# Parameter chain of the state-space part ahead of the feature evictions, upper table levels on VectorE alone

## The chip, the core and the metric

The kernel runs on one core of a Trainium2 chip. The metric is the device time of one launch in microseconds (us). The engines of the core are named as in the profile: PE (TensorE: matrix products and transposes), DVE (VectorE), ACT (ScalarE), POOL (GpSimd) and SP (SyncE, here the issuer of all DMAs). Each runs its own list of instructions in order, and semaphores tie the lists together.

## The reference

One inference step of a one-layer decoder: 256 prompt tokens and 8 x 4 sample tokens, 288 in all, width 1024.

```python
z = rmsnorm(x, norm_g) @ w_in            # [q | k | v | u], each 512 wide
attn = dilated window attention of q, k, v (prompt; samples with a cache of 1024)
dt = exp(log_dt); a_bar = exp((a_re + i a_im) * dt)
b_bar = ((a_bar - 1) / lam) * (b_re + i b_im)
h[t] = a_bar * h[t-1] + b_bar @ u[t];  y[t] = Re(c @ h[t]) + d_skip * u[t]
g = gelu(y); ssm_o = g * sigmoid(g @ w_glu + b_glu)
x = x + [rmsnorm(attn) | rmsnorm(ssm_o)] @ w_out
x = x + moe(rmsnorm(x))                  # top 4 of 32 experts, 1024 -> 2048 -> 1024
y = rmsnorm(x)
```

The state-space part has 32 groups of 16 channels with a complex state of 64 each. All is float32.

## The kernel before

The work is written out by hand, one list for each engine; where two engines meet there is a semaphore `S[...]`, and the order of the lines is the order of the work. `link` makes an engine wait for its own last instruction.

The start. ACT and DVE normalise x into `xn`. PE transposes it in 8 pieces of the width, the "features" j = 0 to 7 (L1036, three transposes each), into four PSUM banks in turn; DVE evicts the even ones (L698), ACT the odd ones (L545), both scaled by `gmx`, into `accT`. So feature j waits for the eviction of feature j − 4. Then PE transposes C and the old states h0 (L1041, L1042, ten transposes) and, when DVE has multiplied the two rows of parameters by dt (L703, L704, semaphore `rows`), the four small parameter rows (L1045, semaphore `prmT`). DVE copies these into `prm` (L707) and reduces the angles to the range of the sine (L708 to L716, semaphore `red`), then evicts h0 (L717) and C (L721, L722). ACT computes the radii (Exp, L550) and cosine and sine (L551, L552, semaphore `exps`).

From there three things run side by side. PE multiplies the features with the four blocks of w_in that give u (`project(0)` to `project(3)`, L1060), and then, in its own order, transposes b_bar (L1070, semaphore `bT_ps`). DVE computes a_bar and b_bar from the parameters (L726 to L754, semaphore `fdone`). POOL builds the angle table `e_tab`, the powers 1 to 128 of the unit factor of a_bar for 16 pairs of groups, by doubling: level L makes 2^L more powers out of the 2^L that are there, with four products, a difference and a sum, on 16 x 2^L elements of each of 128 partitions. POOL does levels 0 to 3 alone (L448 to L458); in levels 4 to 6 POOL does the real part (three operations, L448 to L450) and DVE the imaginary part (L762 to L764), and each level waits for both halves of the one before. Between its levels 5 and 6 DVE copies the transposed b_bar out of PSUM (L771, L772, semaphore `bT`), for which PE waits before the first product of the loop.

The loop over 16 state groups i. PE computes `bu(i)` (b_bar times u, L1082), one turn ahead in two banks; DVE turns it by the table (L786 to L791), runs the scans over time in two halves (L796 to L807) and turns back the low half; POOL turns back the high half (L508 to L513); PE multiplies with C (`c_h(i)`, L1103). Between them PE does the other twelve blocks of the projection, the key and value transposes and the first sample scores. Behind the loop come the attention of prompt and samples, the gated unit, the output projection, the router and the experts, whose 402 MB of weights are fetched in pieces of 1 MB; the first of these loads are issued when the attention is done (`pv`).

Two lines of the angle table on DVE, as they stand before:

```python
for level in (4, 5):
    angle_level(level).then_inc(S["etab_d"], 1)
```

Of the kernel before, what the change touches and what calls it, by code (L numbers as in the profile page):

```python
# [26 lines left out]
ALU = mybir.AluOpType  # L27
ACT = mybir.ActivationFunctionType
# [72 lines left out]
def decoder_step(nc, I, O):  # L101

    with ExitStack() as ctx:
# [85 lines left out]
        def s5_buf(n):  # L189
# [46 lines left out]
            gex ysv b1z b1 b2 etab_p etab_d etab_v gmx con_rest sc osel o_ev yfin  # L236
# [190 lines left out]
        def _(pool):  # L427
# [12 lines left out]
            for level in range(7):  # L440
# [5 lines left out]
                if level >= 5:  # L446
                    pool.wait_ge(S["etab_d"], level - 4)
                link(tt(t1, re, cr, ALU.mult))  # L448
                link(tt(t2, im, ci, ALU.mult))
                ins = tt(e_tab[:, 0, :, m:2 * m], t1, t2, ALU.subtract)  # L450
                if level >= 4:
                    ins.then_inc(S["etab_p"], 1)
                    pool.wait_ge(S["etab_p"], level - 2)
                    continue
                link(ins)
# [3 lines left out]
                if level == 3:  # L459
                    ins.then_inc(S["etab_p"], 1)  # L460
                    pool.wait_ge(S["etab_p"], 1)
                else:
                    link(ins)
# [60 lines left out]
        def _(act):  # L524
# [17 lines left out]
            act.wait_ge(S["gmx"], 16)  # L542
            for n, j in enumerate(range(1, J, 2)):
                act.wait_ge(S["xT_ps"], j + 1)
                A(accT[:, j, :], ps[:, 4 + j % 4, 0:NTOK], ACT.Copy, scale=gmx[:, j:j + 1]).then_inc(S["xT_a"], 1)  # L545
            act.wait_ge(S["prm"], 16 * NPRM)
            A(ld[0:NI, 0:2], ld[0:NI, 0:2], ACT.Exp).then_inc(S["dt"], 1)

            act.wait_ge(S["red"], 1)
            A(prm[:, PA_R, :], prm[:, PA_RD, :], ACT.Exp)  # L550
            A(prm[:, PA_C, :], prm[:, 11, :], ACT.Sin)  # L551
            A(prm[:, PA_S, :], prm[:, 12, :], ACT.Sin).then_inc(S["exps"], 1)  # L552

# [119 lines left out]
        def _(dve):  # L673
# [21 lines left out]
            dve.wait_ge(S["gmx"], 16)  # L695
            for j in range(0, J, 2):
                dve.wait_ge(S["xT_ps"], j + 1)
                ts(accT[:, j, :], ps[:, 4 + j % 4, 0:NTOK], gmx[:, j:j + 1], None, ALU.mult).then_inc(S["xT_d"], 1)  # L698

# [7 lines left out]
            link(dve.tensor_copy(prm[:, 0:4, :], ps[:, 0, 0:64].rearrange("p (a i) -> p a i", a=4)))  # L707
# [8 lines left out]
            ts(two, two, PI_IN, -PI_IN, ALU.min, ALU.max).then_inc(S["red"], 1)  # L716
            link(dve.tensor_copy(h0[:, :, :], ps[:, 1, 0:2 * P].rearrange("p (r n) -> p r n", r=2)))  # L717
# [38 lines left out]
            def angle_level(level):  # L756

                m = 1 << level
                dve.wait_ge(S["etab_p"], level - 3)
                re, im = e_tab[:, 0, :, 0:m], e_tab[:, 1, :, 0:m]  # L760
                t1, t2 = (e_tmp_v[:, a].rearrange("p (i t) -> p i t", i=NI)[:, :, 0:m] for a in range(2))
                tt(t1, re, bc(e_tab[:, 1, :, m - 1:m], [P, NI, m]), ALU.mult)  # L762
                link(tt(t2, im, bc(e_tab[:, 0, :, m - 1:m], [P, NI, m]), ALU.mult))
                return tt(e_tab[:, 1, :, m:2 * m], t1, t2, ALU.add)  # L764

            dve.wait_ge(S["fdone"], 1)
            for level in (4, 5):
                angle_level(level).then_inc(S["etab_d"], 1)
                dve.wait_ge(S["etab_d"], level - 3)
            dve.wait_ge(S["bT_ps"], 1)  # L770
            dve.tensor_copy(bT[:, 0, :], ps[:, 0, :])  # L771
            dve.tensor_copy(bT[:, 1, :], ps[:, 1, :]).then_inc(S["bT"], 1)  # L772
            angle_level(6).then_inc(S["etab_v"], 1)
            dve.wait_ge(S["late"], 16 * 5)

            dve.wait_ge(S["etab_p"], 4)
# [249 lines left out]
        def _(pe):  # L1026
# [5 lines left out]
            for j in range(J):  # L1032
# [4 lines left out]
                ins.then_inc(S["xT_ps"], 1)  # L1037
            pe.wait_ge(S["prm"], 16 * NPRM)
            for r in range(2):
                for b in range(4):  # L1040
                    tp(ps[:, 2 + r, P * b:P * b + P], cnat[:, r, b, :], ident)  # L1041
# [410 lines left out]
```

## Time and profile before

| | |
|---|---|
| device time, three runs | 1430.23, 1430.82, 1434.66 us; median 1430.82 |
| the profiled execution | 1433.22 us, its span from first to last instruction 1431.4 us |
| mean granted clock of TensorE | 0.932 |
| PE busy | 1197.0 us (84%) |
| DVE busy | 574.9 us (40%) |
| ACT busy | 226.4 us (16%) |
| POOL busy | 93.6 us (7%) |
| chain that ended last | PE 61%, DMA 10%, SP's queue 9%, DVE 8% |

Shares over the whole span say little about the start, since most of the span is the experts. The change touches the first 60 us, so the timeline of that stretch is what to read: a row gives the start of an instruction (or of a few alike), its length, the engine and line, and in brackets how long the engine stood idle before it and what released it.

### The profile page before, as it was taken

Reading aid. Unit: us, or ns where it says so; the run is one execution under the profiler, and the core shown is the slowest. Engines: PE = TensorE matmul, PEld = TensorE weight load, DVE = VectorE, ACT = ScalarE, POOL = GpSimd, SP = SyncE. Lnnn points to the kernel's source line nnn. Section 1 sums busy time; section 2 is a strip of 40 time slices with the busy share of each in tenths; the row PEclk is TensorE's granted clock in tenths of the full one; section 3 lists DMA queues with packets and bytes.
Section 4 is the critical chain, followed back from the end, with each engine's and each line's share of the span. In section 5 each row is a group of like instructions: output and inputs, shape, how many; then the busy total and the mean of one; then the engine's idle time right before and its main releaser. Section 6 shows DMA issues by size and latency. Waiting matters only on the chain.

```text
span 1431.4 us, 25686 instructions
## 1 busy us (share of the span) xinstructions
PE 1197.0 (84%) x8896; PEld 477.7 (33%) x8897; DVE 574.9 (40%) x1305; ACT 226.4 (16%) x433; POOL 93.6 (7%) x189
## 2 busy tenths in 40 slices
PE   6998778886998688999889888898998966689965
PEld 4665445534332122333223222333332311223321
DVE  4899622234443233333343333443343322234324
ACT  3002433011111011111111111111111101011112
POOL 1668200000000000000000000000000000000000
PEclk9899878885999999999999999999999988899988
DMA  8225482530479999988978997999639999988893
GB/s 256 102 74 187 158 290 65 231 127 9 173 307 424 424 423 423 424 372 336 423 312 352 391 424 287 423 424 425 272 168 398 423 423 424 424 369 344 349 422 151
DMA packets 77902, 444.94 MB, mean 311 GB/s; under 512 B 16560, under 2 KB 17392, under 8 KB 26640
## 3 DMA queue, kind: packets, MB, share of 16 engines
q1 hardware_dynamic: 77872, 444.56, 76.5%
q8 instruction: 17, 0.28, 0.1%
q14 instruction: 13, 0.11, 0.0%
HBM read 442.02 MB, written 2.51 MB: 311 GB/s over the span
## 4 chain that ended last, share of the span: by engine, by line
PE 61%; DMA 10%; SPq 9%; DVE 8%; issue 7%; DVEq 2%; ACT 1%; POOL 1%; ACTq 0%
PE ps L1355 19%; SPq L402 9%; PE ps L1341 9%; DMA ring<-in_w_moe_dram 7%; PE ps L1364 7%; PE ps L1371 5%; PE ps L1291 3%; PE ps L1383 3%; PE ps L1060 3%; DMA uni<-in_w_moe_dram 2%; PE ps L1379 1%; PE ps L1396 1%; PE ps L1130 1%; DVE uni L1007 1%; PE ps L1328 1%
## 5 line engine op out<-in xcount | busy, mean ns | idle before, releaser
L1355 PE MATMUL ps<-ring,uni 128*32 128x512 f32 x2240 | 253.4, 596 | 10.8 <-DMA ring<-in_w_moe_dram 10.8
L977 DVE TENSOR_TENSOR x<-x,ps 128x1024 f32<-128x1024 f32 x158 | 186.7, 1209 | 6.6 <-PE ps L1341 3.4
L1341 PE MATMUL ps<-uni 64*128 64x512 f32 x632 | 173.6, 655 | 5.2 <-DVE uni L972 2.6
L1371 PE MATMUL ps<-uni 128*32 128x256 f32 x1224 | 92.5, 443 | 85.9 <-issue 85.9
L998 DVE TENSOR_SCALAR uni<-ps 128x256 f32<-128x256 f32 x51 | 21.7, 425 | 341.9 <-PE ps L1355 341.9
L1364 PE MATMUL ps<-ring,uni 128*32 128x512 f32 x1120 | 130.4, 599 | 31.8 <-DVE uni L1007 18.1
L1355 PEld LDWEIGHTS ps<-ring,uni 128*32 128x32 f32 x2240 | 71.4, 110 | 182.3 <-issue 157.1
L654 ACT ACTIVATE uni<-uni 128x256 f32<-128x256 f32 x51 | 21.2, 417 | 539.6 <-DVE uni L998 539.6
L1371 PEld LDWEIGHTS ps<-uni 128*32 128x32 f32 x1224 | 40.9, 123 | 151.9 <-issue 139.0
L1341 PEld LDWEIGHTS ps<-uni 64*128 64x128 f32 x632 | 55.7, 198 | 105.5 <-issue 100.8
L654 ACT ACT_TABLE_LOAD x51 | 65.4, 1283 | 80.5 <-issue 80.1
L987 DVE COPY uni<-ps 128x256 f32<-128x256 f32 x51 | 21.7, 425 | 135.7 <-PE ps L1371 135.7
L1060 PE MATMUL ps<-accT,ring 128*128 128x288 f32 x256 | 68.8, 427 | 0.0
L1364 PEld LDWEIGHTS ps<-ring,uni 128*32 128x32 f32 x1120 | 31.7, 109 | 104.6 <-issue 53.3
L1355 PE MATMUL ps<-tmp,uni 128*32 128x512 f32 x512 | 61.2, 593 | 2.8 <-DMA tmp<-in_w_moe_dram 2.8
L982 DVE TENSOR_TENSOR uni<-con,uni 128x96 f32 (+1 forms) x51 | 13.2, 259 | 122.4 <-issue 122.4
L658 ACT ACTIVATE uni<-ps 128x256 f32<-128x256 f32 x51 | 19.5, 383 | 230.0 <-PE ps L1364 230.0
L1060 PEld LDWEIGHTS ps<-accT,ring 128*128 128x128 f32 x256 | 49.9, 199 | 16.9 <-issue 3.3
L1383 PE MATMUL ps<-kv_rows,uni 128*32 128x512 f32 x408 | 54.6, 607 | 0.0
L1291 PE MATMUL ps<-ring,mixer 128*128 128x512 f32 (+1 forms) x96 | 43.4, 614 | 0.5 <-DVE st L904 0.5
L1007 DVE COPY uni<-ps 128x256 f32<-128x256 f32 x51 | 21.7, 425 | 48.6 <-PE ps L1402 48.6
L991 DVE TENSOR_TENSOR uni<-uni 128x96 f32<-128x96 f32 x204 | 38.5, 251 | 0.0
(317 smaller groups left out, 1172.9 us busy)
## 6 DMA issues: line engine op xcount, KB each, us to landing
ring<-in_w_moe_dram SPq DMA_DIRECT2D x258, 1024.0 KB, 20.2
tmp<-in_w_moe_dram SPq DMA_DIRECT2D x42, 1024.0 KB, 17.8
accT<-in_w_moe_dram SPq DMA_DIRECT2D x21, 1024.0 KB, 19.7
mixer<-in_w_moe_dram SPq DMA_DIRECT2D x21, 1024.0 KB, 21.2
w_glu<-in_w_moe_dram SPq DMA_DIRECT2D x21, 1024.0 KB, 22.8
uni<-in_w_moe_dram SPq DMA_DIRECT2D x21, 1024.0 KB, 24.4
ring<-in_w_in_dram SPq DMA_DIRECT2D x4, 2048.0 KB, 13.0
ring<-in_cache_k_dram SPq DMA_DIRECT2D x8, 1024.0 KB, 5.0
```

The costliest lines, as they stand in the source:

```text
L402: sp.dma_start(slot(turn, k), piece(e + later, k2)).then_inc(landed(turn, k), 16)
L654: A(sig, glu_b, ACT.Sigmoid, scale=ALPHA).then_inc(S["sgm"], 1)
L977: tt(rows(t), rows(t), ps[0:TILES[t][1], b0:b0 + 2, :], ALU.add).then_inc(S["acc"], 1)
L991: ins = tt(selg[:, :, q, :], sel, gb, ALU.mult)
L1007: dve.tensor_copy(mt, ps[:, 3, 0:NQ].rearrange("p (m c) -> p m c", c=P)).then_inc(S["mt"], 1)
L1060: ins = mm(ps[:, 4 + n % 2, 0:NTOK], w_in[:, c // 4, j, P * (c % 4):P * (c % 4) + P], accT[:, j, :], start=(j == 0), stop=(j == J - 1))
L1291: ins = mm(ps[0:n, b0 + 2 * a + c, :], src[:, kb, t0:t0 + n], w_out[:, 4 * a + kb, 512 * c:512 * c + 512], start=(kb == 0), stop=(kb == 3))
L1341: ins = mm(ps[:, b0 + c, :], selT[rows, P * t:P * t + P], y[rows, :], start=True, stop=True)
L1355: ins = mm(hidden(q), xe[:, k % 2, quarter(k // 2)], columns(slot(turn, k), q), start=False, stop=(k == 7), skip_group_check=True)
L1364: ins = mm(ps[quarter(2 * c + m), 4, :], mt[:, m, quarter(k - 8)], slot(turn, k)[:, at:at + 512], start=(k == 8), stop=(k == 11), skip_gro ...
L1371: ins = mm(ps[quarter(q), 2, 0:NQ], sel[:, t, :], h[:, t, NQ * q:NQ * q + NQ], start=(t == 0), stop=(t == 2), skip_group_check=True)
L1383: mm(hidden(q), pick, columns(b1_rows, q), start=True, stop=False, skip_group_check=True)
```

## The change

Four edits. On DVE the even evictions of features move from ahead of the parameter chain to behind the range reduction. On PE the parameter transposes move between features 3 and 4, and C and h0 behind feature 7, with a new semaphore `cps` for DVE's eviction of h0. On ACT the Exp of dt and the Exp of the radii (which gets its own semaphore `prmc`) move ahead of the odd evictions, and cosine and sine between features 3 and 5. In the table, levels 4 to 6 are done whole by DVE, six operations each, behind the copies of b_bar; POOL stops at level 3.

```diff
 # POOL
-            for level in range(7):
+            for level in range(4):
...
-                if level >= 5:
-                    pool.wait_ge(S["etab_d"], level - 4)
                 link(tt(t1, re, cr, ALU.mult))
                 link(tt(t2, im, ci, ALU.mult))
-                ins = tt(e_tab[:, 0, :, m:2 * m], t1, t2, ALU.subtract)
-                if level >= 4:
-                    ins.then_inc(S["etab_p"], 1)
-                    pool.wait_ge(S["etab_p"], level - 2)
-                    continue
-                link(ins)
+                link(tt(e_tab[:, 0, :, m:2 * m], t1, t2, ALU.subtract))
 # ACT
-            act.wait_ge(S["gmx"], 16)
-            for n, j in enumerate(range(1, J, 2)):
+            def features_out(j):
                 act.wait_ge(S["xT_ps"], j + 1)
                 A(accT[:, j, :], ps[:, 4 + j % 4, 0:NTOK], ACT.Copy, scale=gmx[:, j:j + 1]).then_inc(S["xT_a"], 1)
+
             act.wait_ge(S["prm"], 16 * NPRM)
             A(ld[0:NI, 0:2], ld[0:NI, 0:2], ACT.Exp).then_inc(S["dt"], 1)
-
+            act.wait_ge(S["prmc"], 1)
+            A(prm[:, PA_R, :], prm[:, PA_RD, :], ACT.Exp)
+            act.wait_ge(S["gmx"], 16)
+            features_out(1)
+            features_out(3)
             act.wait_ge(S["red"], 1)
-            A(prm[:, PA_R, :], prm[:, PA_RD, :], ACT.Exp)
             A(prm[:, PA_C, :], prm[:, 11, :], ACT.Sin)
             A(prm[:, PA_S, :], prm[:, 12, :], ACT.Sin).then_inc(S["exps"], 1)
+            features_out(5)
+            features_out(7)
 # DVE
-            dve.wait_ge(S["gmx"], 16)
-            for j in range(0, J, 2):
-                dve.wait_ge(S["xT_ps"], j + 1)
-                ts(accT[:, j, :], ps[:, 4 + j % 4, 0:NTOK], gmx[:, j:j + 1], None, ALU.mult).then_inc(S["xT_d"], 1)
...
             ts(two, two, PI_IN, -PI_IN, ALU.min, ALU.max).then_inc(S["red"], 1)
+            dve.wait_ge(S["gmx"], 16)
+            for j in range(0, J, 2):
+                dve.wait_ge(S["xT_ps"], j + 1)
+                ts(accT[:, j, :], ps[:, 4 + j % 4, 0:NTOK], gmx[:, j:j + 1], None, ALU.mult).then_inc(S["xT_d"], 1)
+
+            dve.wait_ge(S["cps"], 1)
             link(dve.tensor_copy(h0[:, :, :], ps[:, 1, 0:2 * P].rearrange("p (r n) -> p r n", r=2)))
...
-                tt(t1, re, bc(e_tab[:, 1, :, m - 1:m], [P, NI, m]), ALU.mult)
-                link(tt(t2, im, bc(e_tab[:, 0, :, m - 1:m], [P, NI, m]), ALU.mult))
-                return tt(e_tab[:, 1, :, m:2 * m], t1, t2, ALU.add)
-
-            dve.wait_ge(S["fdone"], 1)
-            for level in (4, 5):
-                angle_level(level).then_inc(S["etab_d"], 1)
-                dve.wait_ge(S["etab_d"], level - 3)
+                t3, t4 = (e_tmp[:, a, :, 0:m] for a in range(2))
+                tt(t1, re, cr, ALU.mult)
+                tt(t2, im, ci, ALU.mult)
+                tt(t3, re, ci, ALU.mult)
+                link(tt(t4, im, cr, ALU.mult))
+                tt(e_tab[:, 0, :, m:2 * m], t1, t2, ALU.subtract)
+                return tt(e_tab[:, 1, :, m:2 * m], t3, t4, ALU.add)
+
             dve.wait_ge(S["bT_ps"], 1)
             dve.tensor_copy(bT[:, 0, :], ps[:, 0, :])
             dve.tensor_copy(bT[:, 1, :], ps[:, 1, :]).then_inc(S["bT"], 1)
+            dve.wait_ge(S["fdone"], 1)
+            dve.wait_ge(S["etab_p"], 1)
+            link(angle_level(4))
+            link(angle_level(5))
             angle_level(6).then_inc(S["etab_v"], 1)
 # PE
-            for j in range(J):
+            def features(j):
...
+            for j in range(4):
+                features(j)
             pe.wait_ge(S["prm"], 16 * NPRM)
-            for r in range(2):
-                for b in range(4):
-                    tp(ps[:, 2 + r, P * b:P * b + P], cnat[:, r, b, :], ident)
-                tp(ps[:, 1, P * r:P * r + P], h0row[:, r, :], ident)
             pe.wait_ge(S["rows"], 1)
             for a, src in enumerate((par[0:NI, 0:P], par[0:NI, P:2 * P], st_out[0:NI, 0, :], st_out[0:NI, 1, :])):
                 ins = tp(ps[:, 0, NI * a:NI * a + NI], src, ident[0:NI, 0:NI])
             ins.then_inc(S["prmT"], 1)
+            for j in range(4, J):
+                features(j)
+            for r in range(2):
+                for b in range(4):
+                    tp(ps[:, 2 + r, P * b:P * b + P], cnat[:, r, b, :], ident)
+                ins = tp(ps[:, 1, P * r:P * r + P], h0row[:, r, :], ident)
+            ins.then_inc(S["cps"], 1)
```

On DVE, from the last step of b_bar (written into `tmp`) to the first instruction of the loop (reading `ps`), before; `ring` holds the temporaries and b_bar transposed, `uni` the table:

```order
L754 TENSOR_TENSOR tmp<-ring 64x16x16
L762 TENSOR_TENSOR ring<-uni 128x16x16
L763 TENSOR_TENSOR ring<-uni 128x16x16
L764 TENSOR_TENSOR uni<-ring 128x16x16
L762 TENSOR_TENSOR ring<-uni 128x16x32
L763 TENSOR_TENSOR ring<-uni 128x16x32
L764 TENSOR_TENSOR uni<-ring 128x16x32
L771 COPY ring<-ps 128x512
L772 COPY ring<-ps 128x512
L762 TENSOR_TENSOR ring<-uni 128x1024
L763 TENSOR_TENSOR ring<-uni 128x1024
L764 TENSOR_TENSOR uni<-ring 128x16x64
```

And the same place of the changed kernel, up to the middle of level 5:

```order
L753 TENSOR_TENSOR tmp<-ring 64x16x16
L770 COPY ring<-ps 128x512
L771 COPY ring<-ps 128x512
L762 TENSOR_TENSOR ring<-uni 128x16x16
L763 TENSOR_TENSOR ring<-uni 128x16x16
L764 TENSOR_TENSOR tmp<-uni 128x16x16
L765 TENSOR_TENSOR tmp<-uni 128x16x16
L766 TENSOR_TENSOR uni<-ring 128x16x16
L767 TENSOR_TENSOR uni<-tmp 128x16x16
L762 TENSOR_TENSOR ring<-uni 128x16x32
L763 TENSOR_TENSOR ring<-uni 128x16x32
L764 TENSOR_TENSOR tmp<-uni 128x16x32
```

The two copies of b_bar (COPY ring<-ps) moved ahead of levels 4 and 5, and each level has six operations instead of three.

On PE, the start of the changed kernel from feature 3 to the projection (L1068); before, the rows of `par` and `st_out` (the parameter transposes) stand directly ahead of the projection, and no row stands between the features:

```order
L1046 MATMUL ps<-con,par 128x16 x2
L1046 MATMUL ps<-con,st_out 128x16 x2
L1038 MATMUL ps<-con,uni 128x128 x2
...
L1052 MATMUL ps<-con,tmp 128x128 x4
L1053 MATMUL ps<-con,h0row 128x128
L1052 MATMUL ps<-con,tmp 128x128 x4
L1053 MATMUL ps<-con,h0row 128x128
L1068 MATMUL ps<-accT,ring 128x288 x32
```

Features 4 to 7 and the transposes of C (`tmp`) and h0 (`h0row`) now stand between the parameter transposes and the projection.

## Rows read from the trace of the kernel before

**Rows 1.** The chain of waits in order of time: start, us, what.

```profile
45.91 2.08 PE ps L1082 x8
...
103.93 1.07 PE ps L1082 x4
```

**Rows 2.** By stretch: length, busy PE, PEld, DVE, ACT, POOL, clock, DMA.

```profile
44.70:54.80 10.10, 8.89 (x79) 7.59 (x80) 10.07 (x5) 0.00 (x0) 8.79 (x4) 0.50 0.04 14
55.00:105.00 50.00, 50.00 (x199) 33.06 (x197) 47.88 (x122) 4.61 (x10) 28.04 (x62) 1.00 0.16 53
```

**Rows 3.** Timelines of DVE and PE, the loop and its end.

```profile
55.01 0.69 DVE L786 TENSOR_TENSOR ring<-ps,uni 128x512 f32<-128x512 f32 x1 [0.20 <-DVE uni L764]
...
97.75 1.13 PE L1082 MATMUL ps<-uni,ring 32*128 32x256 f32 x4
...
104.43 0.46 DVE L807 TENSOR_TENSOR_SCAN ring<-prm,ring 128x128 f32<-128x128 f32 x1
105.00 0.69 DVE L786 TENSOR_TENSOR ring<-ps,uni 128x512 f32<-128x512 f32 x1
...
160.02 1.02 PE L1103 MATMUL ps<-ring 128*32 128x256 f32 x4 [1.16 <-POOL ring L513]
```

**Rows 4.** Timelines of all engines, 13 to 56 us.

```profile
13.76 6.97 PE L1036 MATMUL ps<-con,uni 128*128 128x128 f32 x24 [13.76 <-DVE uni L693]
...
23.42 0.39 PE L1045 MATMUL ps<-con,par 16*128 16x16 f32 x2 [0.37 <-DVE st_out L704]
23.96 17.57 PE L1060 MATMUL ps<-accT,ring 128*128 128x288 f32 x64
...
25.72 0.42 DVE L717 COPY ring<-ps 128x256 f32<-128x256 f32 x1
...
27.48 0.20 ACT L552 ACTIVATE prm<-prm 128x16 f32<-128x16 f32 x1
...
32.69 0.49 DVE L754 TENSOR_TENSOR tmp<-ring 64x256 f32<-64x256 f32 x1
...
37.87 0.45 POOL L458 TENSOR_TENSOR uni<-tmp 128x128 f32<-128x128 f32 x1
...
41.36 1.04 PE L1070 MATMUL ps<-con,tmp 128*128 128x128 f32 x8
...
44.56 0.69 DVE L771 COPY ring<-ps 128x512 f32<-128x512 f32 x1
...
45.77 2.92 DVE L762 TENSOR_TENSOR ring<-uni 128x1024 f32<-128x1024 f32 x1
45.91 2.08 PE L1082 MATMUL ps<-uni,ring 32*128 32x256 f32 x8 [3.51 <-DVE ring L772]
...
51.56 3.25 DVE L764 TENSOR_TENSOR uni<-ring 128x1024 f32<-128x1024 f32 x1
```

**Rows 5.** SP's small loads issued between 9 and 11 us.

```profile
L303 SPq DMA_DIRECT2D tmp<-in_ssm_c_im_dram x2: 507/507/507, 9.4 to 9.9; - x2
...
DMA to landing us min/median/max: 2.5/2.6/3.1
```

**Rows 6.** Durations: timelines, and one group by line (count, busy us, mean ns).

```profile
14.78 0.52 DVE L698 TENSOR_SCALAR accT<-ps,vec 128x288 f32<-128x288 f32 x1 [1.17 <-PE ps L1036]
...
40.94 0.69 DVE L762 TENSOR_TENSOR ring<-uni 128x512 f32<-128x512 f32 x1
41.55 1.53 DVE L763 TENSOR_TENSOR ring<-uni 128x512 f32<-128x512 f32 x1
...
51.38 9.75 PE L1060 MATMUL ps<-accT,ring 128*128 128x288 f32 x32
...
56.40 0.43 DVE L790 TENSOR_TENSOR ring<-ring 128x256 f32<-128x256 f32 x1
...
62.12 4.15 PE L1060 MATMUL ps<-accT,ring 128*128 128x288 f32 x16
...
L896 DVE TENSOR_TENSOR uni<-mixer 128x1152 f32<-128x1152 f32 x1 | 1.4, 1358 | 0.0
```

More of the change, by code:

```diff
@@ L235, in decoder_step @@
             wo_ps x2 ss3 ms3 rt3 h hT_ps lg rout posps posm cntr gT_ps gT b2ps acc0 chain_a chain_v chain_p
-            gex ysv b1z b1 b2 etab_p etab_d etab_v gmx con_rest sc osel o_ev yfin
+            gex ysv b1z b1 b2 etab_p etab_v prmc cps gmx con_rest sc osel o_ev yfin
             sel selg pick gath xs xeT_ps xe hid glin sgm swc midr selT_ps selT mt_ps mt out_ps y comb acc
@@ L460, in _ @@
                     ins.then_inc(S["etab_p"], 1)
-                    pool.wait_ge(S["etab_p"], 1)
                 else:
@@ L706, in _ @@
             dve.wait_ge(S["prmT"], 1)
-            link(dve.tensor_copy(prm[:, 0:4, :], ps[:, 0, 0:64].rearrange("p (a i) -> p a i", a=4)))
+            dve.tensor_copy(prm[:, 0:4, :], ps[:, 0, 0:64].rearrange("p (a i) -> p a i", a=4)).then_inc(S["prmc"], 1)
+            dve.wait_ge(S["prmc"], 1)
             link(ts(prm[:, 11, :], prm[:, PA_TH, :], TWO_PI / 4, None, ALU.add))
@@ L758, in angle_level @@
                 m = 1 << level
-                dve.wait_ge(S["etab_p"], level - 3)
                 re, im = e_tab[:, 0, :, 0:m], e_tab[:, 1, :, 0:m]
+                cr, ci = (bc(e_tab[:, r, :, m - 1:m], [P, NI, m]) for r in range(2))
                 t1, t2 = (e_tmp_v[:, a].rearrange("p (i t) -> p i t", i=NI)[:, :, 0:m] for a in range(2))
-                tt(t1, re, bc(e_tab[:, 1, :, m - 1:m], [P, NI, m]), ALU.mult)
-                link(tt(t2, im, bc(e_tab[:, 0, :, m - 1:m], [P, NI, m]), ALU.mult))
-                return tt(e_tab[:, 1, :, m:2 * m], t1, t2, ALU.add)
-            dve.wait_ge(S["fdone"], 1)
-            for level in (4, 5):
-                angle_level(level).then_inc(S["etab_d"], 1)
-                dve.wait_ge(S["etab_d"], level - 3)
+                t3, t4 = (e_tmp[:, a, :, 0:m] for a in range(2))
[5 more added lines that the diff above has]
+                return tt(e_tab[:, 1, :, m:2 * m], t3, t4, ALU.add)
             dve.wait_ge(S["bT_ps"], 1)
@@ L772, in _ @@
             dve.tensor_copy(bT[:, 1, :], ps[:, 1, :]).then_inc(S["bT"], 1)
+            dve.wait_ge(S["fdone"], 1)
+            dve.wait_ge(S["etab_p"], 1)
+            link(angle_level(4))
+            link(angle_level(5))
             angle_level(6).then_inc(S["etab_v"], 1)
             dve.wait_ge(S["late"], 16 * 5)
-            dve.wait_ge(S["etab_p"], 4)
             dve.wait_ge(S["etab_v"], 1)
```

## Prediction

> **What bounds the kernel now.** The change lies in the first 60 us, so the question is which engine carries the time from there to the end. I read the chain of waits first. From 45.9 to 105.0 us it names PE alone, and DVE only from then on [rows 1]. The busy time by stretches makes that doubtful: from 55 to 105 us PE is busy 50.0 of 50.0 us and DVE 47.9 of 50.0 [rows 2]. So I went to DVE's own timeline around 105.0. The loop over the 16 state groups begins there with L786. At 105.00 it is the ninth turn (i = 8), and it needs the product bu(8), which PE had ended by 98.9. DVE's last instruction of the turn before, the scan L807, ended at 104.43 + 0.46 = 104.89 [rows 3]. The reader is to see that DVE went on 0.1 us after its own work and had waited for nobody; the product that PE happened to end at 104.99 is the one for the next turn. From its first L786 at 55.01 on, DVE goes from turn to turn in this way, and the tail behind it passes from POOL to PE at 160.02 [rows 3]. So the loop is DVE's, and the number to work out is the moment of DVE's first L786: 55.01 now. Whatever moves it moves all behind it, since the sample scores, the attention, the output projection and the experts each wait for the last, and the expert weights are only fetched once the attention is through.
>
> What sets 55.01? Backwards along DVE [rows 4]: the last table level (L762 to L764) runs from 45.77 to 54.81, behind the two bT copies (44.56 to 45.77), behind levels 4 and 5 (38.4 to 44.5), and these waited for POOL's level 3, which ended at 37.87 + 0.45 = 38.32. PE had the transposes of bT ready at 42.40, so the copies came 2.2 us late, because DVE stood in level 5. In the present kernel the table is the bound here, and DVE fills PE's projection time with two of its levels.
>
> **The change, part by part.**
>
> The parameter chain moves up. The transposes of the parameters stand behind features 0 to 3 instead of behind all eight and the ten c and h0 transposes. A feature is 6.97 / 8 = 0.87 us on PE, so they start at 13.76 + 3.48 = 17.24 instead of 23.42 [rows 4]. What feeds them is early enough: SP issued the last of the small loads at 9.9 and such loads land within 3.1 us, so by 13.0 [rows 5], and the exponential table is fetched while DVE still scales x. The Sin results, at 27.68 now, come 6.2 us or a little more earlier (ACT has the Exp of the radii done by then), at 21.2, and POOL's levels 0 to 3, 10.6 us of work (27.7 to 38.3), end at 31.8 instead of 38.3. This is what the edit gains: 6.5 us on the table's lower levels.
>
> The features pay for it. DVE's first eviction stands behind the range reduction: from the parameter transposes to the point where L717 stands now is 25.72 − 23.42 = 2.30 us, so it starts at 17.24 + 2.30 = 19.54 and ends 0.52 later [rows 4, 6], at 20.06. Feature 4 on PE waits for it (it would have started at 17.2); behind it in PE's queue are features 5 to 7, the c and h0 transposes and the projection. Four features: 20.1 + 3.48 = 23.6. The ten transposes: they end at 23.42 − 0.37 = 23.05 today, 2.3 us behind the last feature (13.76 + 6.97 = 20.73); less the 0.1 us in which neighbours overlap, the projection starts at 25.8, against 23.96. That is 1.8 us later. Its weights are no limit: the present kernel starts on them at 23.96 without a wait.
>
> The projection of the four u blocks. It takes 41.36 − 23.96 = 17.40 us now, and its end is what DVE now waits for. It holds a slow first part: 64 records at the rate of the loop's blocks (16 in 4.15 us) would be 16.6 us; at the rate of the pair at 51.38 (32 in 9.75 us, most of it at a granted clock of 0.50, which is the 1.2 GHz level) they would be 19.5 [rows 2, 6]. I take 17.0, between 16.6 and 17.4, because PE enters it straight from 2.3 us of transposes without a pause, where it now has one of 0.37 us behind them [rows 4]. So it ends at 42.8, within 42.4 to 45.3.
>
> The Trainium skill (TensorE: Matmul & The Clock Gate, Part 1) says that the moment at which the clock rises is not tied to the kernel's start and differs between runs of one kernel. By it the 17.4 us is one draw out of 16.6 to 19.5 and may differ from run to run; no row of a single execution can show that.
>
> What DVE does then. The parameter arithmetic (L726 to L754) ends at 33.2 today. Its start now hangs on the c and h0 transposes, which come 2.8 us later (25.9 instead of 23.05), but DVE reaches h0 at 26.0 against 25.72 and need not wait for Sin any more, so it ends at about 33.2 still. Then DVE stands at the bT copies, which the new order puts ahead of all three levels. POOL's table lies ready from 31.8, and nothing in DVE's queue can use it: from 33.2 DVE waits for PE's bT transposes, 42.8 + 1.04 = 43.9. This wait of 10.7 us is the price of the new order. Where now 6.1 us of levels 4 and 5 lie under the projection, afterwards none does. Both copies take 45.77 − 44.56 = 1.21: 45.1.
>
> The three levels on DVE alone, six operations each. Without POOL beside it a 128x256 operation takes 0.43 us, 128x512 0.69, and 128x1152 1.36 [rows 6]; between the last two the slope gives 128x1024 as 1.22. Neighbours that don't depend on each other overlap by 0.08. So a level is six durations less four overlaps (0.32), and 0.04 at each of two links: 2.34, 3.90 and 7.08, together 13.3 us, and 0.2 as now between the last level and L786. L786 starts at 45.1 + 13.5 = 58.6, against 55.01: 3.6 us later. With POOL beside it the same operations are far dearer (L763 on 128x512 takes 1.53 [rows 6], L762 on 128x1024 2.92 [rows 4]), and this is what moving them gives back: 18 operations in 13.3 us, where half of them take 15 now. But the half that POOL did is added, and the cover is gone. The bounds: 3.2 us with a projection of 16.6, 6.1 with one of 19.5.
>
> PE comes out level. bu(0) waits for the second copy, which ends at 45.85 now and at about 45.2 then; PE loses its present stop of 3.51 us [rows 4] but gains nothing by it: it has no idle time in the loop to 105 us now, with DVE 3.6 us later it waits for the results of DVE and POOL, as it does at 160.02 [rows 3]. The loop itself is untouched; its DVE operations keep their durations. The other moved instruction, the Exp of the radii on ACT, is 0.2 us and lies ahead of the two ACT evictions, which PE does not miss before 20.9.
>
> The sum: 1.8 (projection starts later) − 0.4 (its slow part) + 1.04 and 1.21 unchanged, 58.6 − 55.0 = 3.6 us. The profiled execution took 1433.22 us with a span of 1431.4; the sum makes that 1436.8. The median of the runs shown is 1430.82, on which the prediction stands: 1434.4. The three runs spread over 4.4 us, mostly by one, so 0.3% (4.3 us) is about what a measurement can tell from no change, and my sum lies just under it.
>
> **The rivals.**
>
> PE is the bound, as the chain of waits has it. Then what counts is bu(0), which starts 0.6 us earlier, and PE's clock: its stop before bu(0) shrinks from 3.5 to 1.3 us, so the 0.50 from 44.7 to 54.8 us may not come, and the pair at 51.38 would take 8.3 instead of 9.75, the small products before it perhaps 2 us less. That is 0.6 + 1.5 + 2 and a little, 4 to 5 us faster, 1426.3; it decides from the point where DVE shows an idle gap at each L786. Against it: the 0.1 us gap at 105.00, and the product ready since 98.9. Chance 0.08.
>
> The slow part is long, or DVE's levels are dearer than alone. A projection near 19.5 us, or strided writes into the table that cost more than the 128x512 read, put L786 at 60 to 61: 5 to 6 us slower, 1436.5. For it speaks the new pause of PE between 17.8 and 20.1; against it that the reads of level 5 took 0.69 on the same strides. Chance 0.2.
>
> The delay is given back. A later stage, such as the key and value loads between 105 and 157 us or the first expert weights, might be waited for now by a margin that I took for none; then 0 to 2 us remain, 1431.8. The tail at 160.02 that waits for POOL speaks against it. Chance 0.12.
>
> **How the numbers follow.** The forecast, 3.6 us and one to either side for the estimates of durations (1433.4 to 1435.4), has 0.6. Of it a third lies over the bound of 4.3. So slower: 0.2 and 0.18, 0.38; faster 0.08; within the bound the rest, 0.54. The range takes in the dear levels and most of what is given back, and half the spread of the runs: 1430.4 to 1438.2.
>
> **What would show it.** In the changed profile: parameter transposes on PE near 17.2 and features 4 to 7 from 20.1; POOL's level 3 done near 31.8; a wait of DVE of about 10.7 us for PE's bT transposes; 18 level operations in 13.3 us with 0.7 and 1.2 us for the 512 and 1024 wide; L786 first at 58.6; turns of the loop as long as now; PE idle ahead of c_h(0) for POOL. I am wrong if the first L786 comes 3.6 us late and the span does not, or if it comes at 55 or before because the projection or the levels are much cheaper.

## The result, and the profile after

The changed kernel takes 1437.11 us (median of 12 runs, 1431.66 to 1440.77) against 1431.73 (12 runs, 1429.67 to 1434.66) of the kernel before: ratio 1.0033, 95% interval 1.002 to 1.0046. A second set gave 1437.55 against 1431.96, ratio 1.0044 (1.0032 to 1.0057). So it is slower, by 0.3 to 0.4%, 5 to 6 us. I had forecast 3.6 us, 1434.4, and given "slower by over 0.3%" a chance of 0.38 against 0.54 for "within". The mechanism came as forecast, with the wait of DVE mis-sized; a part of the time has no cause found.

The profiled execution took 1436.42 us, with a span of 1434.6. Timelines of the changed kernel, all engines, from the first feature to the first turn of the loop and at its end; the rows answer to [rows 3, 4]:

```profile
13.80 3.51 PE L1038 MATMUL ps<-con,uni 128*128 128x128 f32 x12 [13.80 <-DVE uni L690]
17.12 0.37 PE L1046 MATMUL ps<-con,par 16*128 16x16 f32 x2
...
19.96 3.54 PE L1038 MATMUL ps<-con,uni 128*128 128x128 f32 x12 [2.26 <-DVE accT L713]
...
25.62 16.20 PE L1068 MATMUL ps<-accT,ring 128*128 128x288 f32 x64
...
29.96 0.48 POOL L451 TENSOR_TENSOR uni<-tmp 128x128 f32<-128x128 f32 x1
...
33.38 0.42 DVE L753 TENSOR_TENSOR tmp<-ring 64x256 f32<-64x256 f32 x1
...
41.66 1.04 PE L1078 MATMUL ps<-con,tmp 128*128 128x128 f32 x8
...
42.73 0.69 DVE L770 COPY ring<-ps 128x512 f32<-128x512 f32 x1 [8.93 <-PE ps L1078]
...
44.05 0.42 DVE L762 TENSOR_TENSOR ring<-uni 128x256 f32<-128x256 f32 x1
44.07 1.14 PE L1090 MATMUL ps<-uni,ring 32*128 32x256 f32 x8 [1.38 <-DVE ring L771]
...
55.98 1.22 DVE L767 TENSOR_TENSOR uni<-tmp 128x1024 f32<-128x1024 f32 x1
57.29 0.69 DVE L787 TENSOR_TENSOR ring<-ps,uni 128x512 f32<-128x512 f32 x1
...
162.26 1.02 PE L1111 MATMUL ps<-ring 128*32 128x256 f32 x4 [1.17 <-POOL ring L505]
```

The reader is to see four things. POOL's level 3 ends at 30.44, 7.9 us earlier than before, and lies there. DVE ends the parameter arithmetic at 33.80 and stands still for 8.93 us, until PE has b_bar transposed. Then come the copies and the three levels, 13.2 us from 44.05 to the first loop instruction. And the loop starts at 57.29 instead of 55.01, 2.28 later, and the C product behind it stands at 162.26 instead of 160.02, 2.24 later: the loop itself is as long as before.

Busy time of the changed kernel by stretches, with the columns of [rows 2]:

```profile
55.00:105.00 50.00, 45.73 (x174) 29.72 (x173) 47.97 (x116) 3.28 (x8) 28.00 (x61) 0.97 0.16 53
```

PE, which was busy all of these 50 us before, is busy for 45.7 now; DVE's 48.0 has not changed.

### The profile page after: what moved, and what is told of

Its sections match the earlier page's. It is cut to its first block, busy times and chain, and to the rows that moved or that the text cites. A ratio compares the mean times of both kernels' runs of the same rounds, so it can differ in the third digit from the quotient of the medians.

```text
span 1434.6 us, 25682 instructions
## 1 busy us (share of the span) xinstructions
PE 1197.6 (83%) x8896; PEld 475.3 (33%) x8897; DVE 573.6 (40%) x1314; ACT 226.3 (16%) x433; POOL 78.4 (5%) x180
## 4 chain that ended last, share of the span: by engine, by line
PE 56%; DMA 11%; DVE 11%; SPq 8%; issue 7%; DVEq 2%; ACT 1%; POOL 0%; ACTq 0%
PE ps L1363 19%; DMA ring<-in_w_moe_dram 9%; PE ps L1349 9%; SPq L402 8%; PE ps L1372 7%; PE ps L1379 5%; PE ps L1299 3%; PE ps L1391 3%; DMA uni<-in_w_moe_dram 2%; PE ps L1387 1%; PE ps L1404 1%; PE ps L1138 1%; DVE uni L1008 1%; DVE ring L787 1%; PE ps L1336 1%
## 5 line engine op out<-in xcount | busy, mean ns | idle before, releaser
L1068 PE MATMUL ps<-accT,ring 128*128 128x288 f32 x256 | 69.1, 428 | 0.0
L983 DVE TENSOR_TENSOR uni<-con,uni 128x96 f32 (+1 forms) x51 | 13.2, 259 | 125.3 <-issue 125.3
L1068 PEld LDWEIGHTS ps<-accT,ring 128*128 128x128 f32 x256 | 50.1, 200 | 17.1 <-issue 3.3
## 6 DMA issues: line engine op xcount, KB each, us to landing
tmp<-in_w_moe_dram SPq DMA_DIRECT2D x42, 1024.0 KB, 17.6
```

The lines of the kernel that those rows point to most:

```text
L1068: ins = mm(ps[:, 4 + n % 2, 0:NTOK], w_in[:, c // 4, j, P * (c % 4):P * (c % 4) + P], accT[:, j, :], start=(j == 0), stop=(j == J - 1))
```

## The experiments

For each kernel I note three marks of its profile in us: the start of the first loop instruction on DVE, the start of the last C product behind the loop on PE, and the span. Each ratio is against runs of the kernel before that were taken beside it; below, a ratio is turned into a time by multiplying its distance from 1 by their median, about 1432 us.

| kernel | first loop instruction | C product | span | ratio to before (95%) |
|---|---|---|---|---|
| before | 55.01 | 160.02 | 1431.4 | |
| changed | 57.29 | 162.26 | 1434.6 | 1.0033 (1.002 to 1.0046) |
| front_only | 50.80 | 156.00 | 1430.0 | 0.9993 (0.9984 to 1.0002) |
| table_only | 57.39 | 162.36 | 1435.6 | 1.001 (1.0001 to 1.0018) |
| levels_first | 50.42 | 155.44 | 1426.2 | 0.9988 (0.9979 to 0.9997) |
| early_evict | 55.62 | 160.64 | 1435.0 | 1.0016 (1.0004 to 1.0029) |
| dve_delay | 58.64 | 163.92 | 1436.1 | one run |
| pe_delay | 55.11 | 162.37 | 1433.7 | one run |
| best | 46.29 | 153.06 | 1427.3 | 0.9985 (0.9974 to 0.9996) |
| after_again | 57.42 | 163.40 | 1431.3 | 1.0044 (1.0032 to 1.0057) |
| dve_delay_long | 69.23 | 174.24 | 1444.1 | 1.011 (1.0094 to 1.0126) |
| best_again | 46.53 | 154.99 | 1430.6 | 0.9971 (0.9958 to 0.9983) |
| after_warm | 57.42 | 162.48 | 1437.3 | 1.0015 (1.0001 to 1.0029) |
| best_warm | 44.33 | 152.75 | 1427.8 | 0.9965 (0.9953 to 0.9977) |

My theory A: DVE carries the time from its first loop instruction on, and what the change costs is the place of the copies of b_bar ahead of all three levels. Its rivals: PE carries the loop, as the chain of waits says; or the late features cost.

### The two halves of the change: front_only and table_only

`front_only` is the changed kernel with the table of before, on POOL too:

```diff
+            dve.wait_ge(S["fdone"], 1)
+            for level in (4, 5):
+                angle_level(level).then_inc(S["etab_d"], 1)
+                dve.wait_ge(S["etab_d"], level - 3)
             dve.wait_ge(S["bT_ps"], 1)
...
-            link(angle_level(4))
-            link(angle_level(5))
             angle_level(6).then_inc(S["etab_v"], 1)
```

> The new order of the start alone: parameter chain ahead of the feature evictions as in the changed kernel, but the table built as before (POOL and DVE share levels 4 to 6, DVE does 4 and 5 ahead of the copies of b_bar). Theory A (DVE carries the time from the first loop instruction on, and the new place of the copies is what costs): POOL's level 3 done near 30.4, DVE's levels 4 and 5 from 33.8 to 40.0 under the projection, copies at 42.7 to 44.1 depending on how quick the projection is, level 6 shared for 9.0 us, first loop instruction at 53.2 to 54.6 against 55.0 before and 57.3 in the changed kernel; the time 0.4 to 1.8 us under before. Rival B (the late features and the late projection cost): the time follows the projection, 1.7 us over before.

DVE's timeline:

```profile
35.06 0.43 DVE L769 TENSOR_TENSOR ring<-uni 128x256 f32<-128x256 f32 x1
...
42.68 0.69 DVE L778 COPY ring<-ps 128x512 f32<-128x512 f32 x1 [2.78 <-PE ps L1084]
43.28 0.68 DVE L779 COPY ring<-ps 128x512 f32<-128x512 f32 x1
43.88 2.17 DVE L769 TENSOR_TENSOR ring<-uni 128x1024 f32<-128x1024 f32 x1
45.97 3.37 DVE L770 TENSOR_TENSOR ring<-uni 128x1024 f32<-128x1024 f32 x1
49.37 1.23 DVE L771 TENSOR_TENSOR uni<-ring 128x1024 f32<-128x1024 f32 x1
50.80 0.69 DVE L793 TENSOR_TENSOR ring<-ps,uni 128x512 f32<-128x512 f32 x1 [0.20 <-DVE uni L771]
```

Levels 4 and 5 lie under the projection again, and the loop starts 4.2 us earlier than before, more than the 0.4 to 1.8 I expected. The difference is level 6. I had taken it at the 9.0 us of before, but here POOL had begun its half at 41.10, 2.8 us ahead of DVE, and was through at 48.26, so DVE's last operation ran alone in 1.23 us where it took 3.25 before [rows 4], and the level took DVE 6.7 us. The rival falls: the projection begins at 25.59, 1.6 us late, and the loop is not later for it. In the time only about 1 us of the 4.2 appears (the interval reaches from −2.3 to +0.3 us, so the time alone does not show a gain); more on that below.

`table_only` is the kernel before with the table edit alone:

```diff
-            for level in (4, 5):
-                angle_level(level).then_inc(S["etab_d"], 1)
-                dve.wait_ge(S["etab_d"], level - 3)
...
             dve.tensor_copy(bT[:, 1, :], ps[:, 1, :]).then_inc(S["bT"], 1)
+            dve.wait_ge(S["fdone"], 1)
+            dve.wait_ge(S["etab_p"], 1)
+            link(angle_level(4))
+            link(angle_level(5))
```

> The table edit alone: start in the old order, levels 4 to 6 whole on DVE behind the copies of b_bar. Theory A: copies at 41.1 to 42.4 (not held up any more), then 13.3 us of levels, first loop instruction at 55.8 to 57.1, the time 0.7 to 2.1 us over before although nothing of the start moved. Rival B (late features): no change or faster, since POOL is out of DVE's way and PE's first loop product comes 2.2 us earlier.

```profile
42.83 0.69 DVE L763 COPY ring<-ps 128x512 f32<-128x512 f32 x1 [9.52 <-PE ps L1064]
...
57.39 0.69 DVE L780 TENSOR_TENSOR ring<-ps,uni 128x512 f32<-128x512 f32 x1
```

With the start in its old order DVE stands for 9.52 us ahead of the copies, and the loop starts 2.4 us late, at 57.39; so theory A holds here, though by 0.3 us more than its range, since the projection took 17.7. The loss comes with the new table alone, and the two halves don't add: the new start alone gains 4.2 us at this place, the new table alone loses 2.4, both together lose 2.3. Once all three levels wait for PE's transposes, what the new start gives POOL is worth nothing.

### The cover given back: levels_first

```diff
+            dve.wait_ge(S["fdone"], 1)
+            dve.wait_ge(S["etab_p"], 1)
+            link(angle_level(4))
+            link(angle_level(5))
             dve.wait_ge(S["bT_ps"], 1)
             dve.tensor_copy(bT[:, 0, :], ps[:, 0, :])
             dve.tensor_copy(bT[:, 1, :], ps[:, 1, :]).then_inc(S["bT"], 1)
-            dve.wait_ge(S["fdone"], 1)
-            dve.wait_ge(S["etab_p"], 1)
-            link(angle_level(4))
-            link(angle_level(5))
```

> The changed kernel with one edit: levels 4 and 5 on DVE stand ahead of the copies of b_bar, in the gap in which DVE waited 8.9 us for PE's transposes. Theory A: levels 4 and 5 run from 33.8 to 40.0, the copies start where they did (42.7 to 44.1), level 6 takes 7.1, first loop instruction at 51.2 to 52.6, 6.1 us earlier than in the changed kernel for the same projection and 2.4 to 3.8 earlier than before; the C product behind the loop (160.02 before, 162.26 in the changed kernel) at 156.2 to 157.6. Theory PE (the chain of waits is right and PE carries the loop): the product moves by no more than PE's first loop product does, so it stays at 162.3 as in the changed kernel, since PE starts the loop at the same time in both.

```profile
33.54 0.42 DVE L762 TENSOR_TENSOR ring<-uni 128x256 f32<-128x256 f32 x1
...
38.95 0.69 DVE L767 TENSOR_TENSOR uni<-tmp 128x512 f32<-128x512 f32 x1
42.11 0.69 DVE L774 COPY ring<-ps 128x512 f32<-128x512 f32 x1 [2.47 <-PE ps L1078]
...
50.42 0.69 DVE L787 TENSOR_TENSOR ring<-ps,uni 128x512 f32<-128x512 f32 x1
```

Four lines moved, and the loop starts at 50.42, 6.9 us earlier than in the changed kernel: 6.1 us of levels 4 and 5 went into the gap (33.54 to 39.64), and this profile's projection was 0.5 us shorter, which also puts the start below the range that I had given. The C product moved by 6.8, while PE's first loop product came only 0.6 us earlier (43.45 against 44.07). So in the changed kernel PE does not carry the loop. The ratio falls from 1.0033 to 0.9988. Against `front_only`, where POOL does half of the same levels under the same cover, the loop starts 0.4 us earlier, and from the copies on it is 8.3 us against 8.1: the move of POOL's half to DVE costs next to nothing, its place in the queue does.

### Who carries the loop: dve_delay and pe_delay

`dve_delay` puts three fills (memsets of 128x1024, whose result nothing reads) ahead of the loop on DVE:

```diff
+            for _ in range(3):
+                link(dve.memset(ssm_g[:, :, :, :, :], 0.0))
             for i in range(NI):
```

> The kernel before with three extra fills of 128x1024 (about 0.9 us each, 2.8 in all) on DVE right ahead of the first loop instruction; PE's list is untouched. Theory A (DVE carries the loop from its first instruction): the loop starts 2.8 us later and the C product behind it stands at 162.8 instead of 160.02. Theory PE (the chain's reading, PE carries it to 105 us): the product moves by much less, 0 to 1 us, since PE starts the loop when it did.

`pe_delay` doubles the products for the samples on PE:

```diff
             def bu_samples():
-                for i in range(NI):
+                for i in list(range(NI)) * 2:
```

> The kernel before with the 32 small products for the samples done twice (about 3.5 us more on PE, same results), ahead of the blocks of the projection in the loop; DVE's list is untouched. Theory A: DVE's turns wait for PE's C products two turns back, which are early by 1.4 us at turn 2 and by 0.7 at turn 5 as I read the timelines, so the first 0.7 us of the delay cost nothing and the product behind the loop moves by about 2.5 to 3 us: PE is no more than 0.7 us from carrying the loop. Theory PE: the full 3.5 us. If PE has wide slack: 0.

A fill cost 1.19 us with its link, not 0.9, so `dve_delay` shifted DVE by 3.6 us (58.64); the C product stood at 163.92, 3.9 us later than before. The whole delay arrived, with PE's list untouched. In `pe_delay` the doubled products cost PE 3.4 us (64 records in 3.68 before, 128 in 7.09), and DVE's timeline shows what PE in the lead looks like:

```profile
55.11 0.69 DVE L786 TENSOR_TENSOR ring<-ps,uni 128x512 f32<-128x512 f32 x1 [0.20 <-DVE uni L764]
...
70.90 0.42 DVE L796 TENSOR_TENSOR_SCAN ring<-prm,ring 128x128 f32<-128x128 f32 x1 [1.84 <-PE ps L1103]
...
77.02 0.42 DVE L796 TENSOR_TENSOR_SCAN ring<-prm,ring 128x128 f32<-128x128 f32 x1 [0.36 <-POOL ring L513]
```

The idle time stands ahead of the scan, not ahead of the turn; in before no such wait stands at a scan. The stretch from the first loop instruction to the C product became 2.25 us longer (107.26 against 105.01), so the first 1.2 of the 3.4 us cost nothing; from my timelines I had read 0.7. The kernel before is thus carried by DVE, with PE 1.2 us behind it. That part of my theory stands, and so does a limit for it: a DVE that starts earlier soon meets PE. In `front_only` and `levels_first` it has just done so: each has one scan with a wait, of 0.33 and 0.22 us.

### The late features: early_evict

```diff
+            dve.wait_ge(S["gmx"], 16)
+            for j in (0, 2):
+                dve.wait_ge(S["xT_ps"], j + 1)
+                ts(accT[:, j, :], ps[:, 4 + j % 4, 0:NTOK], gmx[:, j:j + 1], None, ALU.mult).then_inc(S["xT_d"], 1)
             dve.wait_ge(S["prmT"], 1)
...
-            dve.wait_ge(S["gmx"], 16)
-            for j in range(0, J, 2):
+            for j in (4, 6):
...
-            act.wait_ge(S["prmc"], 1)
-            A(prm[:, PA_R, :], prm[:, PA_RD, :], ACT.Exp)
             act.wait_ge(S["gmx"], 16)
             features_out(1)
             features_out(3)
+            act.wait_ge(S["prmc"], 1)
+            A(prm[:, PA_R, :], prm[:, PA_RD, :], ACT.Exp)
```

> The changed kernel with one edit at the start: DVE evicts features 0 and 2 and ACT features 1 and 3 in their idle time ahead of the parameter transposes (DVE stood idle for 3.69 us there, ACT for 5.15). Theory A: feature 4 on PE no longer waits 2.26 us, the projection starts 2.2 us earlier (23.4), the rest of DVE's row moves with it, first loop instruction 2.2 us earlier, at 55.1 with a projection as quick as in the changed kernel (16.0) and 56.5 with one of 17.4; the time about as before the change. Rival: the weights of the projection or the parameter chain, now 0.1 us later, take over and less than half of it arrives.

```profile
17.50 0.37 PE L1049 MATMUL ps<-con,st_out 16*128 16x16 f32 x2
17.80 3.54 PE L1041 MATMUL ps<-con,uni 128*128 128x128 f32 x12
...
23.46 16.70 PE L1071 MATMUL ps<-accT,ring 128*128 128x288 f32 x64
...
41.07 0.69 DVE L773 COPY ring<-ps 128x512 f32<-128x512 f32 x1 [8.97 <-PE ps L1081]
...
55.62 0.69 DVE L790 TENSOR_TENSOR ring<-ps,uni 128x512 f32<-128x512 f32 x1
```

PE's wait of 2.26 us is gone and the projection starts 2.2 us earlier; it took 0.5 us longer than in the changed kernel, so 1.7 us arrive at the loop. That is what the new start costs as long as everything hangs on the projection. In the time, where I had expected about none over before, 2.3 us are left (ratio 1.0016).

### Both repairs: best, and whether a shift arrives

`best` has the early evictions, levels 4 and 5 ahead of the copies, and three of the four products of level 6 too (`bt_copies` is the wait for bT_ps and the two copies):

```diff
                 tt(t3, re, ci, ALU.mult)
+                if level == 6:
+                    bt_copies()
                 link(tt(t4, im, cr, ALU.mult))
```

> Both repairs together and one more: features 0 to 3 evicted early, levels 4 and 5 and three of the four products of level 6 on DVE ahead of the copies of b_bar. Theory A: projection from 23.4, transposes of b_bar done at 40.5 to 41.9, DVE busy with the table from 31.5 to 41.2, copies to 42.5 to 43, first loop instruction at 46 to 47, about 8.5 us ahead of before. PE's first loop product comes only 3 to 3.5 us ahead of before, so by the slack of 0.7 us PE takes over in the loop and the C product behind it moves by 4 to 6 us against before (154 to 156); the time 0.3 to 0.4% under before. Theory PE: 3 to 3.5 us. If DVE alone counted: 8.5 us.

The loop starts at 46.29, 8.7 us ahead of before, and the C product stands 7.0 us ahead, more than the 4 to 6 I had expected. DVE's rows show PE taking over at the third turn, with the marks of `pe_delay`; the first row is PE's, its first pair of projection blocks in the loop:

```profile
45.65 9.69 PE L1075 MATMUL ps<-accT,ring 128*128 128x288 f32 x32
46.29 0.69 DVE L794 TENSOR_TENSOR ring<-ps,uni 128x512 f32<-128x512 f32 x1
...
61.58 0.42 DVE L804 TENSOR_TENSOR_SCAN ring<-prm,ring 128x128 f32<-128x128 f32 x1 [1.36 <-PE ps L1118]
...
67.70 0.42 DVE L804 TENSOR_TENSOR_SCAN ring<-prm,ring 128x128 f32<-128x128 f32 x1 [0.36 <-POOL ring L505]
```

That pair ends at 55.34, 5.8 us earlier than before (51.38 + 9.75 = 61.13 [rows 6]); with the 1.2 us that PE had in hand this makes the 7.0.

But the time was only 2.1 us under before, where I had expected 0.3 to 0.4%. Here a second question came up: the three kernels with an earlier loop had gained 4.0, 4.6 and 7.0 us at the C product and showed 1.0, 1.7 and 2.1 in the time; the changed kernel had lost 2.2 and showed 4.7. So I asked whether a shift arrives whole, with twelve fills instead of three, and ran two kernels again.

> The kernel before with 12 fills on DVE ahead of the first loop instruction, 1.19 us each with their links, 14.3 us in all. It asks whether a shift of the loop's start arrives whole at the end. Theory whole: first loop instruction at 69.3, the C product behind the loop at 174.4, the time 14 to 14.7 us over before (ratio 1.0098 to 1.0103). Rival (the experts' stage, which waits for the weights, gives part of it back): as the three faster starts suggest, of which 4.0, 4.6 and 7.0 us at the C product only 1.0, 1.7 and 2.1 us came out in the time; a third to a half, ratio 1.004 to 1.006.

> The changed kernel once more, in the same call as the two below. Its profile showed only 2.3 us more at the start of the loop and 3.2 more in the span, while its runs were 4.7 us over before. Theory noise: the difference is spread of the runs (they vary by 9 us), and a second set lies nearer to the shift of the loop's start, 2.3 to 3.9 us (ratio 1.0016 to 1.0027) depending on how long the projection takes (16.0 to 17.9 us in the profiles so far). Rival (a later stage adds to the delay): again 1.0033 with about 2 us more than the loop's shift in the stages behind the loop.

> The kernel with early evictions and the table levels ahead of the copies once more. Its C product behind the loop stood 7.0 us earlier than before, its time only 2.1 us. Theory whole (the shift arrives and the first set was spread): ratio near 0.995 to 0.9965. Theory given back: again 0.998 to 0.999, with the stage of the experts longer than before in the profile by 2 us or more.

`dve_delay_long` shifts the C product by 14.2 us and the time by 15.8 (13.5 to 18.0 by the interval): of a later loop nothing is given back behind it. It does not tell the same of an earlier loop. `best_again` gave 0.9971, 4.2 us for 5.0 at the C product, between the two theories; its profile has 1275.6 us from the C product to the end of the span, against 1271.4 in before, as the theory of giving back had said.

The second set of the changed kernel refutes the theory that the first was spread: 1.0044, where it gave 1.0016 to 1.0027. It was further from its profile than the first: 6.3 us, where the loop starts 2.4 us late. Its profile shows one place that can add. At the end of its loop PE was in the lead:

```profile
145.61 0.81 PE L1111 MATMUL ps<-ring 128*32 128x256 f32 x3 [2.01 <-POOL ring L505]
...
161.47 1.05 PE L1111 MATMUL ps<-ring 128*32 128x256 f32 x4
163.40 1.03 PE L1111 MATMUL ps<-ring 128*32 128x256 f32 x4
```

The last C product has no wait for POOL ahead of it, as it has in the others, and comes 1.1 us later than in the first profile. The granted clock from 130 to 165 us was 0.85 there (0.50, the 1.2 GHz level, from 146.6 to 156.7), against 0.95 in both the first profile and the kernel before. Yet the stages behind the loop were quicker in that execution and its span was 1431.3, so this one profile does not explain the runs around it, and the rival that a later stage adds about 2 us is not borne out by it either.

### PE kept busy beforehand: after_warm and best_warm

```diff
             pe.wait_ge(S["con"], 16)
+            for _ in range(8):
+                mm(ps[:, 0, 0:2 * P], ident, con[:, 0:2 * P], start=True, stop=True)
             pe.wait_ge(S["xn"], 1)
```

> The changed kernel with eight 128x256 products of constants on PE ahead of the first feature, in the time in which PE waits for x (6.8 to 13.7 us); their result is overwritten unread. In the two sets of the changed kernel the time was 5.4 and 5.6 us over before (medians), but the loop starts only 2.3 and 2.4 us late in its two profiles. Theory clock: with the new order the copies hang on the projection (DVE idle 8.9 us ahead of them), so every run pays for the slow part of its own projection, and the profiles happened to show short ones (16.0 and 16.3 us); with PE busy beforehand the projection is 15.5 in all runs, features go quicker, the loop starts at 54 to 56 and the time falls by 3 to 5 us to 1432.5 to 1434. Rival (the 3 us arise behind the loop or elsewhere): the time falls by no more than the loop's start in the profile does, 1 to 3 us.

> The same eight products ahead of the kernel with early evictions and the levels ahead of the copies (1429.44 and 1428.08 before, C product at 153.1 and 155.0 in its profiles). Theory clock: projection 15.5 and starting a little earlier, but DVE's table work ahead of the copies now ends at 41.4, so only PE's side gains; C product at 152 to 153, time 1426 to 1428. Rival: no change.

PE in the profile of `after_warm`:

```profile
14.04 2.63 PE L1040 MATMUL ps<-con,uni 128*128 128x128 f32 x12 [1.43 <-DVE uni L690]
...
19.17 3.53 PE L1040 MATMUL ps<-con,uni 128*128 128x128 f32 x12 [2.26 <-DVE accT L713]
...
24.81 17.13 PE L1070 MATMUL ps<-accT,ring 128*128 128x288 f32 x64
41.78 1.04 PE L1080 MATMUL ps<-con,tmp 128*128 128x128 f32 x8
```

Features 0 to 3 ran quicker, in 2.63 us against 3.51, but behind the wait of 2.26 us features 4 to 7 took 3.53 again, and the projection, though it started 0.8 us earlier, needed 16.97 us. The granted clock was 0.50 from 18 to 27 us. The loop started at 57.42, no earlier than in the changed kernel, where I had forecast 54 to 56 with a projection of 15.5. The ratio was 1.0015, below the 1.0033 and 1.0044 of the changed kernel, but its interval overlaps that of the first. So it is inconclusive: the loop's start says that the eight products did nothing here, the time says perhaps 3 us. In `best_warm`, where no such wait stands between, features 4 to 7 took 2.81 us, the projection ran from 21.11 for 15.8 us, and the loop started at 44.33. There too the granted clock was 0.50 from 18.5 to 21.5 us, while PE was busy with transposes all the time, so the missing wait alone does not hold it up. This is the fastest kernel of the study, 1427.68 us (ratio 0.9965), about 5 us under before and over 9 under the changed kernel; against `best_again` (0.9971) the difference is within the spread.

## Why the prediction was right, and where it was off

**Who carries the loop.** I held against the chain of waits that DVE does, by the gap of 0.1 us at 105.00. Shown: two delays of DVE moved the C product by their whole amount (3.6 gave 3.9, 14.2 gave 14.2), the four moved lines of `levels_first` by 6.8 of 6.9 us against the changed kernel, and the delay of PE by two thirds. The rival "PE is the bound", with its 4 to 5 us faster, is refuted; that PE is only 1.2 us behind I had not worked out.

**The start on PE and ACT.** Parameter transposes were to start at 17.24 (17.12), the eviction at 19.54 (19.39), feature 4 at 20.1 (19.96), the projection at 25.8 (25.62). All within 0.2 us. The cost of 1.8 us on PE was 1.66.

**POOL's levels.** To be done at 31.8; they were at 30.44. Sine and cosine came at 20.63, since the fetch of the Sin table began 0.5 us before DVE had reduced the angles, and POOL needed 9.8 us instead of 10.6. It changed nothing, as forecast: DVE used the table only at 44.05.

**The wait of DVE.** 10.7 us forecast, 8.93 measured. This is the term that was mis-sized. What moved the loop is the projection: I took 17.0 us, it took 16.04. Another 0.2 us is its earlier start, and the remaining 0.6 is that DVE's parameter arithmetic ended at 33.80, not 33.2, which cost nothing, since DVE waited behind it. I had bounded the projection by 16.6 as four times a row of the loop (16 records in 4.15 us), which counts the tail of the last record four times. ACT's evictions in before, one behind each block, show the rate without it:

```profile
33.80 0.41 ACT L556 ACTIVATE uni<-ps 128x288 f32<-128x288 f32 x1 [3.47 <-PE ps L1060]
37.68 0.41 ACT L556 ACTIVATE uni<-ps 128x288 f32<-128x288 f32 x1 [3.47 <-PE ps L1060]
```

A block takes 3.88 us, four take 15.5, and that is what `front_only` and `levels_first` needed (15.52). So the loop started at 57.29, below the lowest value I had given (58.2). DVE's own part was right: 13.5 us of levels with the gap to the loop forecast, 13.2 measured, the three sizes 0.42, 0.69 and 1.22 us where I had priced 0.43, 0.69 and 1.22.

**The size of the whole.** 3.6 us forecast, 2.2 in the profile's loop, 3.2 in the spans, 5.4 and 5.6 in the medians of two sets (4.7 and 6.3 by the ratios). That the total was near the forecast is in part luck: a term too large by 1.3 us stands against 2.5 to 3 us that I did not have. And of the 2.7 us between 1434.4 and 1437.11, 0.9 is the base: the three runs before had a median of 1430.82, the twelve one of 1431.73. Where the 2.5 to 3 us arise I can't say. They don't come with the table alone (`table_only`), nor from a later stage that stretches any delay (`dve_delay_long`). Take the ratio as a time and subtract the shift of the C product. In the kernels with the new start that leaves 1.7 us (`early_evict`), 2.5 and 2.9 (changed, two sets), 2.9 (`levels_first`), 3.0 (`front_only`), 4.8 and 0.9 (`best`, two sets); with the old start −0.9 (`table_only`) and +1.5 (`dve_delay_long`). Each has an interval of one to two us to either side, so one alone says little, but the sign is the same in all seven sets. They are less independent than that sounds, since all subtract the mark of the one profile of before. With PE busy beforehand it is −0.3 (`after_warm`) and 2.3 (`best_warm`). That runs without a profile have a slower projection or a slower clock in the loop than the profiled ones would fit, and `after_warm` leans that way; so does the spread within a set, in which the fastest of the twelve runs of the changed kernel (1431.66 us) had a mean granted clock of 0.933 and the slowest (1440.77 us) one of 0.921. A rival is not excluded: in the table above, span less C product is 1271.6 us in the mean of the five profiles with the old start (1269.9 to 1273.2) and 1273.2 in that of the nine with the new one (1267.9 to 1275.6), so a part may lie behind the loop. Neither is shown, and the cause stays open.

**The sign.** That cover was lost, and not gained, was the step that decided, and the experiments show it: with levels 4 and 5 under the projection (`front_only`, `levels_first`) the loop starts 4.2 and 4.6 us earlier than before, with them behind the copies (`table_only`, changed) 2.4 and 2.3 us later.

## What to carry to other kernels

When work moves from two engines to one, ask first what stands behind it in the new queue and what it waits for: here 13 us of table work was put behind two copies that waited for another engine, and POOL's result lay unused for 13.6 us. Moving four lines up gained 6.9 us. Where the chain of waits names one engine over a long stretch in which a second one is just as busy, look at the gaps ahead of the second engine's instructions, and if in doubt delay each of them by a known amount: here the two delays of DVE came out at the end of the loop to within 0.3 us, where the runs of one kernel spread over 3 to 11. And where two engines are 1 us apart, a gain of one counts only up to that point, unless the other starts earlier too.

## What was not expected of the hardware

The length of the projection differed with the order of the start. In five profiles with the old order, in which the parameter transposes stand directly before it, behind a wait of 0.37 us, its 64 records took 17.40, 17.67, 17.89, 17.42 and 17.39 us. In seven with the new order, in which ten transposes lead into it without a pause, they took 16.04, 15.52, 15.52, 16.53, 16.49, 16.32 and 16.13. The Trainium skill (TensorE: Matmul & The Clock Gate, Part 1) says that the moment of the rise is not tied to the kernel's start and differs from run to run; here the length varied by 0.5 and 1.0 us within an order, while the means of the two orders (17.6 and 16.1) lie 1.5 apart. With PE busy beforehand, in the new order too, it was 15.8 and, behind the wait of 2.26 us, 16.97. Which of the differences between the two orders shortens it was not tested.

How much DVE was slowed beside POOL hung on how far the two ran apart. Its operations on 128x1024 took 2.92, 2.91 and 3.25 us in level 6 of before, where both began within 0.1 us, and 2.17, 3.37 and 1.23 in `front_only`, where POOL was 2.8 us ahead and through before the third; alone they took 1.22 each.
